# Reordering the split and sum work around Strassen chunks, and three products moved to GpSimd

## What is computed

```python
def conv_ffn(h, p, buf):
    u = h @ p['w_ffn_up']
    a, v = u[..., :D_FF], u[..., D_FF:]
    T = a.shape[1]
    ext = jnp.concatenate([buf.astype(a.dtype), a], axis=1)
    w = p['ffn_conv_w']
    c = p['ffn_conv_b'] + sum(ext[:, j:j + T] * w[j] for j in range(CONV_W))
    out = (jax.nn.silu(c) * v) @ p['w_ffn_down']

    f, buf = conv_ffn(rmsnorm(x, p['norm_ffn_pre']), p, conv_buf)
    x = x + rmsnorm(f, p['norm_ffn_post'])
```

## Time and profile before

| | |
|---|---|
| time, median of 3 runs | 1882.58 us (1881.4 to 1882.79) |
| the profiled execution's own time | 1880.04 us |
| its span | 1878.2 us |
| PE busy | 1803.6 us (96%) |
| DVE busy | 1266.8 us (67%) |
| ACT busy | 951.5 us (51%) |
| POOL busy | 230.1 us (12%) |

### The profile page before, as it was taken

One profiled execution on the slowest core, in us unless ns is written; L12 is line 12 of the kernel. 1 busy time (PEld: TensorE's weight loads), 2 busy tenths in 40 slices (PEclk: granted clock), 3 DMA queues, 4 the chain that ended last, 5 costly groups with the idle time before them and its releaser, 6 DMA issues.

```text
span 1878.2 us, 31219 instructions
## 1 busy us (share of the span) xinstructions
PE 1803.6 (96%) x11636; PEld 1650.6 (88%) x11636; DVE 1266.8 (67%) x1973; ACT 951.5 (51%) x1593; POOL 230.1 (12%) x257
## 2 busy tenths in 40 slices
PE   8999999999999999999899999999999999999996
PEld 7999976599999999999799999656988999999994
DVE  5777875435775766678767778654377766757777
ACT  6444546435663544535654445564366543635356
POOL 0000023200112121111000000350001121111200
PEclk9999999999999999999999999999999999999998
DMA  5312121411456666655131112314116666666641
GB/s 183 94 58 70 64 74 42 162 45 57 122 140 148 167 152 156 152 152 145 52 108 49 58 65 68 90 48 138 57 50 153 152 147 155 146 162 161 134 106 62
DMA packets 98902, 204.03 MB, mean 109 GB/s; under 512 B 16864, under 2 KB 35680, under 8 KB 98728
## 3 DMA queue, kind: packets, MB, share of 16 engines
q1 hardware_dynamic: 63952, 144.39, 23.8%
q0 software_dynamic: 21888, 39.86, 13.0%
q10 hardware_dynamic: 12912, 17.78, 2.8%
HBM read 170.98 MB, written 8.65 MB: 96 GB/s over the span
## 4 chain that ended last, share of the span: by engine, by line
PE 56%; DVE 17%; ACT 11%; issue 7%; DMA 6%; POOL 1%; ACTq 0%; DVEq 0%; SPq 0%; POOLq 0%
PE G L799 35%; PE WA L799 12%; PE WB L799 7%; DVE wlo L2167 4%; DMA t<-in_wstream 3%; ACT whi L1484 3%; DVE cc L2167 2%; DVE tmp L2167 2%; PE G L803 1%; DMA wraw<-in_wstream 1%; DVE Y L2167 1%; DMA wraw<-t 1%; ACT sq L1484 1%; ACT cc L1484 1%; PE WB L803 1%
## 5 line engine op out<-in xcount | busy, mean ns | idle before, releaser
L799 PE MATMUL G<-Hh,wlo 128*128 128x328 f32 x1384 | 452.3, 327 | 15.5 <-DVE Hl L2167 8.1
L799 PE MATMUL G<-Hh,whi 128*128 128x328 f32 x1384 | 434.4, 314 | 0.0
L799 PE MATMUL G<-Hl,whi 128*128 128x328 f32 x1384 | 433.0, 313 | 0.0
L799 PEld LDWEIGHTS G<-Hh,wlo 128*128 128x128 f32 x1384 | 261.8, 189 | 31.5 <-DVE Hl L2167 12.0
L799 PEld LDWEIGHTS G<-Hh,whi 128*128 128x128 f32 x1384 | 261.9, 189 | 2.3 <-issue 0.4
L799 PEld LDWEIGHTS G<-Hl,whi 128*128 128x128 f32 x1384 | 261.8, 189 | 0.0
L1484 ACT ACTIVATE whi<-wraw 128x1024 fp32r<-128x1024 f32 (+2 forms) x171 | 155.6, 910 | 200.0 <-PE G L799 113.9
L2167 DVE TENSOR_TENSOR wlo<-wraw,whi 128x1024 fp32r<-128x1024 f32 (+2 forms) x171 | 177.5, 1038 | 61.3 <-ACT whi L1484 49.1
L799 PE MATMUL G<-gh,wlo 128*128 128x328 f32 x424 | 134.2, 316 | 9.6 <-DVE tmp L2167 8.8
L799 PE MATMUL G<-gh,whi 128*128 128x328 f32 x424 | 132.8, 313 | 0.0
L799 PE MATMUL G<-gl,whi 128*128 128x328 f32 x424 | 132.1, 312 | 0.0
(11 more groups left out here) (327 smaller groups left out, 4098.8 us busy)
## 6 DMA issues: line engine op xcount, KB each, us to landing
wraw<-in_wstream SPq DMA_DIRECT2D x108, 512.0 KB, 3.3
wff<-in_wstream SPq DMA_DIRECT2D x40, 512.0 KB, 4.6
t<-in_wstream SPq DMA_DIRECT2D x76, 256.0 KB, 4.6
t<-in_wstream POOLq DMA_DIRECT2D x38, 256.0 KB, 4.7
ckT<-in_ckT SPq DMA_DIRECT2D x12, 512.0 KB, 3.4
wff<-in_wstream POOLq DMA_DIRECT2D x20, 256.0 KB, 4.3
t<-wff POOLq DMA_DIRECT2D x20, 256.0 KB, 3.3
wff<-t POOLq DMA_DIRECT2D x20, 256.0 KB, 5.6
```

What stands on the lines that cost most here:

```text
L799: return pe.matmul(out, lhsT, rhs, start=start, stop=stop, skip_group_check=True)
```

## The change

1. In `down_pass`, the last block of tiles 0 to 2 is done with the twelve matmuls of g's high part first, which wait for `gh`; the six of the low part follow and wait for `gl`. A tile counts as done (`down`) after its low part.
2. In each chunk DVE adds the T1 product to `p` first, and then makes the pending block's `gl`.
3. In block 3 and in the second block of each later group, ACT makes the high parts that stood between its first and second copy into `R` only after the second copy.
4. Around pass 0 ACT makes `Hh` after tiles 1 and 2 and `whi<-t` after tile 3, DVE makes `Hl` and `wlo<-t` ahead of the last four `Sf` sums and `Sl`.
5. SP issues block 3's first loads and sums ahead of piece `P_UP + 2` instead of in their own turn.
6. In the last pass the split of the last down unit (`whi_x`, `wlo_x`) moves from before the tiles to after tile 0's square and scale (ACT) and after tile 1's `acc` (DVE).
7. At the end POOL makes three of the products Y·R (128x656 each, into `Sf`), and DVE only adds them to X.

```diff
--- before.py
+++ after.py
...
-    return S_DVE * l + (13, 14, 19, 21)[i]
+    return S_DVE * l + (13, 14, 21, 16)[i]
...
     return (gh_f, gl_f)[x][:, G4 - 1, :].rearrange("p (k n) -> p k n", k=2)
+def y_by_norm(k):
+    return Sf[:, 0 if k < 6 else 1, k - 2 & 3:(k - 2 & 3) + 2, :]
...
         sp.dma_start(t3[:, :], b22).then_inc(S("t3_in"), 16)
+    def piece_in(l, p):
+        g = l * PIECES + p
+        if earlier[g] is not None:
+            sp.wait_ge(S("w_split"), earlier[g] // PIECES * UNITS_L + last_unit(earlier[g] % PIECES) + 1)
+        for s, lo, hi, at in parts_of(p):
+            sp.dma_start(raw_of(p)[:, at:at + hi - lo], a["wstream"][l, s][:, lo:hi]).then_inc(S(loaded[g][0]), 16)
+        for c, p0 in P_CHUNK.items():
+            if p == p0 + 1:
+                sum_parts(l, c)
...
         p = g % PIECES
-        if earlier[g] is not None:
-            sp.wait_ge(S("w_split"), earlier[g] // PIECES * UNITS_L + last_unit(earlier[g] % PIECES) + 1)
-        if p == P_CHUNK[NPL]:
+        if p == P_UP + 2:
             sp.wait_ge(S("oas_taken"), l + 1)
...
             sp.wait_ge(S("out"), 32 * (l + 1))
-        for s, lo, hi, at in parts_of(p):
-            sp.dma_start(raw_of(p)[:, at:at + hi - lo], a["wstream"][l, s][:, lo:hi]).then_inc(S(loaded[g][0]), 16)
-        for c, p0 in P_CHUNK.items():
-            if p == p0 + 1:
-                sum_parts(l, c)
+            for e in range(P_CHUNK[NPL], P_CHUNK[NPL] + 2):
+                piece_in(l, e)
+        if p not in (P_CHUNK[NPL], P_CHUNK[NPL] + 1):
+            piece_in(l, p)
         if g % PIECES == 6:
...
+    pool.wait_ge(S("rstd_a"), 2 * DEPTH)
+    for k in (2, 4, 6):
+        pool.tensor_tensor(y_by_norm(k), Y[:, k:k + 2, cols_of(0)],
+                           R[:, cols_of(0)].rearrange("p (a n) -> p a n", a=1).broadcast_to([P, 2, HALF]),
+                           ALU.mult).then_inc(S("qpe"), 1)
 @block.tensor
...
-        def block(n, i, to, x):
+        def block(n, i, to, x, parts=(0, 1, 2)):
             f = nk * n + i
...
             pe.wait_ge(S("w_split"), g + 1)
-            if n == 0 and x == 0:
+            if n == 0 and x == 0 and parts[-1] == 2:
                 pe.wait_ge(S("gl"), 2 * (l * KF + c0 + i) + 2)
+            elif n == 0 and x == 0:
+                pe.wait_ge(S("gh"), l * KF + c0 + i + 1)
             wh, wl, h, m = w_hi_of(g)[:, ws], w_lo_of(g)[:, ws], gh[:, (c0 + i) % G4, :], gl[:, (c0 + i) % G4, :]
-            mm(to, wl, h[:, cols_of(x)], i == 0, False)
-            mm(to, wh, h[:, cols_of(x)], False, False)
-            return mm(to, wh, m[:, cols_of(x)], False, i == nk - 1)
+            for k in parts:
+                e = mm(to, (wl, wh, wh)[k], (h, h, m)[k][:, cols_of(x)], i == k == 0, i == nk - 1 and k == 2)
+            return e
...
         for n in range(3):
-            blocks(n, nk - 1, nk)
+            for x in range(2):
+                block(n, nk - 1, bank(down_bank(n), x), x, (0, 1))
+        for n in range(3):
+            for x in range(2):
+                e = block(n, nk - 1, bank(down_bank(n), x), x, (2,))
+            e.then_inc(S("down"), 1)
         if q < NQ - 1:
...
                 carry(pending)
-            highs(l, u0 - 1)
+            if c != NPL:
+                highs(l, u0 - 1)
             after(B11)
...
             halo(c)
-            highs(l, u0 + B21)
+            if c not in (NPL, GROUPS[group_of(c)][0] + 1):
+                highs(l, u0 + B21)
             after(T2)
...
             g_high(last_c)
-            if q == NQ - 1:
-                w_high(l, UNITS_L - 1)
             for n in range(KD):
...
                     did(f(two(Y[:, n, :]), halves(down_bank(n)), ACT.Copy), "act_took")
+                if not q and n in (1, 2):
+                    act.wait_ge(S("tile"), t0 + T_UP + 2 * NPL)
+                    s_high(Hh[:, 2 * n - 2:2 * n, cols_of(1)], s4_part(n - 1), 12, -1.0)
                 if not q and n == 5:
-                    s_high(Sh[:, 0, :, :], Sf[:, 0, :, :], 18)
-                    act.wait_ge(S("tile"), t0 + T_UP + 2 * NPL)
-                    for x in range(2):
-                        s_high(Hh[:, 2 * x:2 * x + 2, cols_of(1)], s4_part(x), 12, -1.0)
-                if q and q < NQ - 1 and nk * (n + 1) % 8 == 0:
-                    highs(l, u0 + nk * (n + 1) // 8 - 1)
-                if not q and n >= 5:
+                    s_high(Sh[:, 0, :, :], Sf[:, 0, :, :], 20)
+                if q < NQ - 1 and nk * (n + 1) % 8 == 0:
                     highs(l, u0 + nk * (n + 1) // 8 - 1)
...
             step(f(Y[:, n, :], Y[:, n, :], ACT.Copy, scale=cols[:, l, C_FFNPOST + n:C_FFNPOST + n + 1]))
+            if n == 0:
+                w_high(l, UNITS_L - 1)
         w_high(l + 1, 0)
...
             lows(l, u0 + T2)
-            if pending is not None:
-                g_low(pending)
             after(T1)
...
             did(tt_(p7[:, :], p7[:, :], bank(G[s], 0), ALU.add), "dve_took")
+            if pending is not None:
+                g_low(pending)
             lows(l, u0 + T1)
...
                 lows(l, u0 - 1)
+                for x in range(2):
+                    s_low(2 + x, Hl[:, 2 * x:2 * x + 2, cols_of(1)], s4_part(x),
+                          Hh[:, 2 * x:2 * x + 2, cols_of(1)], -1.0)
+                lows(l, u0)
                 for k in range(KH):
                     s_sum(Sf[:, 0, k, :], KH + k, 1, Sf[:, 0, k, :])
-                s_low(2, Sl[:, 0, :, :], Sf[:, 0, :, :], Sh[:, 0, :, :])
-                for x in range(2):
-                    s_low(3 + x, Hl[:, 2 * x:2 * x + 2, cols_of(1)], s4_part(x),
-                          Hh[:, 2 * x:2 * x + 2, cols_of(1)], -1.0)
+                s_low(4, Sl[:, 0, :, :], Sf[:, 0, :, :], Sh[:, 0, :, :])
             if q == NQ - 1:
...
                 g_low(last_c)
-            if q == NQ - 1:
-                w_low(l, UNITS_L - 1)
             for n in range(KD if q < NQ - 1 else 3):
...
                         add_square(n0 + N_FFNPOST, n, n == 0)
+                        if n == 1:
+                            w_low(l, UNITS_L - 1)
                 if q < NQ - 1 and nk * (n + 1) % 8 == 0:
...
+    def residual_a(k):
+        dve.wait_ge(S("qpe"), 4 * DEPTH + k // 2)
+        xs = X[:, k:k + 2, cols_of(0)]
+        did(tt_(xs, xs, y_by_norm(k), ALU.add), "x", by=2)
     ffn_out_b(4)
...
     ffn_out_b(KD - 2)
-    residual(0, 2, 2)
+    residual_a(2)
     add_square_b(n0 + N_FFNPOST, KD - 3)
...
     add_square_b(n0 + N_FFNPOST, KD - 2)
-    residual(0, 4, 2)
+    residual_a(4)
     add_square_b(n0 + N_FFNPOST, KD - 1)
-    residual(0, 6, 2)
+    residual_a(6)
     dve.wait_ge(S("rstd"), n0 + N_FFNPOST + 1)
...
```

## The result

The changed kernel takes 1912.06 us (median of 4 runs, 1905.04 to 1914.17) against 1882.68 us (4 runs, 1881.4 to 1884.51). The ratio is 1.0149, with a 95% interval of 1.012 to 1.0177: slower, by 28 us. The forecast was 22.6 us, with a range of 1890 to 1911 us: 1882.6 + 28.0 = 1910.6 lies at its upper edge, and the median of the four runs a little over it. The profiled execution took 1910.59 us, with a span of 1908.8.

The account below looks back on a forecast made before the run. PE, busy 96% of the span, was taken as the bound, so only its gaps could change. The terms summed to +22.6 us on the profiled 1880.0; from the runs' median 1882.6 that gave 1905, range 1890 to 1911.

Parts of the forecast that it names:

- the clock: Last pass, behind the wait at tile 5: low clock costs 1.5 us in layer 1, half in layer 0; +2.2.
- rival E: Block 8 or a pass start: a longer wait lowers the clock, 1.5 us each, four give 1911; chance 0.08.
- edit 1: Passes 1 to 4: tile 3 waits 0.5 us, +4.0, no gain from g's low part; last pass's first add 1.2 later.
- edit 2: Each chunk on DVE: waits for `p` (3.7 us) go, but PE comes earlier to the wait for tmp; -0.8.
- edit 3: Blocks 7, 11, 15: later split delays loads and sum by 1.18 us, +7.1; block 19 +0.4; block 3 +1.0.
- edits 4 and 5: First chunk: ACT starts 3.25 us later with 3.16 less to do, +0.2; the earlier loads give 0.
- edit 6: Last pass, tile 5: splits and the late first add put Y's third add 3.1 us later; two layers, +6.2.
- edit 7: Kernel end: POOL's products block DVE instructions with two SBUF inputs, +4.2, against -1.9 for products moved; sum +2.3.
- Block 3's +1.0: Block 3: the moved high part makes its split and SP's next load about 3.3 us later; 0.5 a layer.

Follow-up runs that it names:

- b1_order: The kernel before with only the last block of tiles 0 to 2 reordered, g's high part first: ratio 1.0042 to the kernel before, +7.9 us.
- u3_splits: The changed kernel with the high parts back ahead of ACT's second copy into `R`: ratio 1.011 to the kernel before, +20.7 us.
- r_early: The kernel before with blocks 7, 11, 15 and 19 splitting earlier, high part ahead of silu, low part ahead of times_v: ratio 0.9984, -3.0 us.

## Why the prediction was right, and where its terms were off

The forecast, slower by 22.6 us, had the direction and most of the causes. That its sum came near is in part luck. Of its 22.6 us, 20.4 were waits and 2.2 the clock; the two profiled executions differ by 15.5 us of idle PE and 12.2 of low clock. So the waits were put too high by about 5 us (some of that is the unusual wait of 2.2 us in the trace of before), and the clock too low by about 10. "More low clock" was rival E, with a chance of 0.08. By the prediction's own steps (each figure of the last column is known to 6 us either way):

| step | forecast | alone in the kernel before | undone in the changed kernel |
|---|---|---|---|
| edit 1 (with its 1.2 us in each last pass) | +6.4 | +7.9 | 11.7 |
| edit 2 | -0.8 | +4.3 | not tried |
| edit 3 | +8.5 | +7.3 (without block 3) | 7.3 |
| edits 4 and 5 | +0.2 | +0.8 | not tried |
| edit 6 (the rest of the last pass) | +6.0 | +5.5 | 9.4 |
| edit 7 | +2.3 | +1.3 | 4.5 |
| sum | 22.6 | 27.1 | |

- **Edit 1.** The 0.5 us came out as 0.49 in each of passes 1 to 4, and nothing waits for g's low part. That is shown by the rows and by both runs. The last pass's share was 0.97 us a layer by the gaps in b1_order and not 1.2.
- **Edit 2 is the step that failed.** "I credit -0.8, and take 0 to -3.7 as the ends": the true value was outside both ends, on the other side. The mechanism was named rightly, PE comes earlier to the same wait for tmp; what was missed is that PE also comes earlier to the waits for `R` ahead of T1 and T2 (1.7 us), and that the clock fell behind the longer wait at the last pass (1.35 us). The credit of 0.8 had no row behind it. That the clock falls there is shown for one execution; about 2 of the 4.3 us have no place.
- **Edit 3.** 7.3 against 7.1 + 0.4 for these blocks, and the agreement is in part luck. In the changed kernel the chain from the split to SP's loads, POOL's sums and ACT is shown by the rows and by u3_splits, and by r_early at block 20 from the other side; but it is worth 5.4 us of waits there, not 8.5, and the rest of u3_splits' gain is low clock (3.9 by its trace) and scatter. In the kernel before, 5.0 us are paid ahead of B22, because the two splits hold up the p add on DVE, a path that the prediction didn't name. Block 3's +1.0 wasn't tried alone; no wait for it shows when the edit is undone.
- **Edits 4 and 5.** Right in the waits, and for the reason given: 3.19 us taken from ACT, as much put ahead of it.
- **Edit 6.** Right in its waits: the last pass's gaps at tiles 3, 4 and 5 grow by 6.2 us in the changed kernel, as forecast. The clock was given 2.2 us and taken by the length of the wait ("a little less than the 3.69 after which its clock was low"); layer 0 kept full clock behind 2.87 us and layer 1 lost it behind 2.51. That way of telling it was wrong, and this is the term that was sized worst: 12.2 us of low clock in the two traces.
- **Edit 7.** Right by its mechanism, smaller in size. The three stretched instructions cost 3.5 us and not 4.2: the first was longer by 0.98, as forecast ("about 1 us"), the other two by 1.30 and 1.21 and not by 1.6 each.
- **The rest, 28.0 against 22.6,** is 4.5 of the parts (5.1 of it edit 2) and 0.9 that isn't in any part alone, far less than the 5 us to which the sum is known. Undone one by one in the changed kernel, edits 1, 6 and 7 give 11.7, 9.4 and 4.5, 10.9 us more than they cost alone, which is about as much as such differences are uncertain. The clock accounts for that much in the traces: undoing them takes 6.2, 4.9 and 4.3 us of low clock away, 15.4 together and so more than the 12.2 that there are, which they can only do by sparing the same stretches. The changed kernel's four executions have a mean granted clock of 0.980 to 0.988, those with one edit undone 0.981 to 0.991, the 59 of the kernel before in the three lots 0.987 to 0.994. That low clock makes up this part of the loss is shown. Which gaps bring which stretch isn't: of those in the changed kernel, the ones at 881.6, 908.9, 1844.2 and 1857.8, absent from the trace of before, come where gaps of several edits add; but the one at 205.8 lies ahead of all edits, and the trace of before has two, at 1201.3 and 1713.3, that the changed kernel's hasn't.

## What to carry to other kernels

Before moving work off a wait, ask what else the moved piece feeds and what stands behind it on the same engine. A weight split that looks like filler may be the event that frees a buffer, and its lateness then travels through load, sum and split to a product a block later (5.4 us in the changed kernel); and it may hold up the next step of its own engine (5.0 us in the kernel before). A short wait removed just ahead of a longer one isn't won: here 5.9 us were taken away and 6.8 came back further on. When PE is busy for 96% of the time, count the low clock as a term of its own: here it was about as large as the waits, and its place couldn't be told from the length of a wait. Moving elementwise work to GpSimd didn't pay here: two instructions of 0.95 us were bought with three that were 1.2 us longer.

## What the runs showed of the hardware

- DVE instructions with two inputs in SBUF took until shortly after the end of the POOL product of two SBUF inputs beside them: 0.50 us became 1.48, 1.80 and 1.71, and 1.50, 1.80 and 1.70 in another program, to 0.02 us the same. `Y<-Y,WB`, one input in PSUM and started 0.05 us ahead of POOL's product, kept its 0.50. POOL's product of 128x656 took 1.60 us, and 1.87 each when it came in turns with DVE's. By the Trainium skill ("SBUF — State Buffer", on who interferes with whom) this is what a shared port held for a whole instruction would do, and the trace agrees: each DVE instruction ended about 0.36 us after POOL's.
- The granted clock behind a wait isn't told by its length: 1.00 after 2.87 us, 0.51 after 2.51 and 0.54 after 1.98, all in one execution.
- Executions of one kernel differ in time as they differ in mean granted clock: the changed kernel took 1905.04 us at 0.988, 1910.59 at 0.983, 1913.53 at 0.980 and 1914.17 at 0.981; the kernel before, in the lot with b1_order, 1875.14 us at 0.994 and 1881.31 at 0.989, its fastest and its slowest.
- A wait for a chain of DMAs differs from one execution to the next: at block 16 of layer 1 the same code waited 2.24 us or not at all.
